# The recurrence's level products, on diagonal blocks of 32 instead of 64

## The reference

```python
def step(S, inp):
    r_t, w_t, k_t, v_t, kk_t, b_t = inp
    sa = jnp.einsum('bhvk,bhk->bhv', S, kk_t)
    S = (S * w_t[:, :, None, :] - sa[..., None] * b_t[:, :, None, :]
         + v_t[..., None] * k_t[:, :, None, :])
    return S, jnp.einsum('bhvk,bhk->bhv', S, r_t)
```

## Time and profile before

| | us |
|---|---|
| median of 3 runs | 3751.14 |
| their range | 3749.05 to 3752.72 |
| the profiled execution's own time | 3751.76 |
| its span, first to last instruction | 3749.9 |
| recurrence, within the span | 821 to 1520 |
| PE busy in the span | 3507.7 |

### The profile page before, as it was taken

The page is one execution under the profiler, slowest core; times in us unless marked ns, Lnnn a source line. Parts: engine busy times, 40 slices in busy tenths (PEclk is TensorE's granted clock), DMA queues, the critical chain, the costliest instruction groups (busy, mean ns, idle before and its releaser), DMA issues.

```text
span 3749.9 us, 63580 instructions
## 1 busy us (share of the span) xinstructions
PE 3507.7 (94%) x28813; PEld 2207.1 (59%) x28813; DVE 1890.8 (50%) x2744; ACT 935.8 (25%) x1858; POOL 49.2 (1%) x114
## 2 busy tenths in 40 slices
PE   7998879989999999799999999998899698999988
PEld 3445655549989898444444444445566345777753
DVE  2038862235555554646555540115999653544524
ACT  3005630125455545220000000100111302233310
POOL 2000000000000000100000000000000000000000
PEclk9999989989999999899999999999999899999999
DMA  6011210000000000222111121113111012010021
GB/s 228 23 42 59 79 68 7 28 6 17 5 18 4 4 4 4 99 84 79 68 62 45 42 92 40 51 56 95 34 34 56 8 66 58 23 34 23 1 84 62
DMA packets 110624, 177.52 MB, mean 47 GB/s; under 512 B 5379, under 2 KB 66562, under 8 KB 109714
## 3 DMA queue, kind: packets, MB, share of 16 engines
q1 hardware_dynamic: 101218, 141.59, 11.2%
q10 hardware_dynamic: 9136, 31.87, 2.4%
HBM read 147.23 MB, written 26.21 MB: 46 GB/s over the span
## 4 chain that ended last, share of the span: by engine, by line
PE 85%; DVE 9%; ACT 3%; DMA 2%; issue 1%; ACTq 0%; SPq 0%; DVEq 0%
PE psum_all L66 84%; ACT sbuf_all L75 3%; DVE sbuf_all L102 3%; DVE sbuf_all L94 3%; DVE sbuf_all L84 2%; PE psum_all L69 1%; ACT L75 1%; DMA sbuf_all<-in_w_mod 1%; DVE sbuf_all L91 0%; DMA sbuf_all<-in_gla_w_out 0%; DVE sbuf_all L108 0%; DVE sbuf_all L90 0%; DMA sbuf_all<-in_w_up 0%; DVE sbuf_all L97 0%; DMA yd_spill<-sbuf_all 0%
## 5 line engine op out<-in xcount | busy, mean ns | idle before, releaser
L66 PE MATMUL psum_all<-sbuf_all 64*64 64x64 f32 (+11 forms) x28042 | 3406.1, 306 | 185.2 <-ACT sbuf_all L75 57.4
L66 PEld LDWEIGHTS psum_all<-sbuf_all 64*64 64x64 f32 (+5 forms) x28042 | 2120.0, 153 | 1449.7 <-issue 1033.3
L75 ACT ACTIVATE sbuf_all<-psum_all 128x512 f32<-128x512 f32 (+5 forms) x925 | 408.2, 461 | 1562.3 <-PE psum_all L66 1435.7
L94 DVE SCALAR_TENSOR_TENSOR sbuf_all<-sbuf_all 128x1040 f32<-128x1040 f32 (+8 forms) x571 | 623.5, 1094 | 25.3 <-PE psum_all L66 4.9
L84 DVE TENSOR_TENSOR sbuf_all<-sbuf_all 128x512 f32<-128x512 f32 (+10 forms) x593 | 470.3, 817 | 167.6 <-ACT sbuf_all L75 123.6
L75 ACT ACTIVATE sbuf_all<-sbuf_all 128x64 f32<-128x64 f32 (+13 forms) x451 | 260.3, 587 | 855.4 <-DVE sbuf_all L78 354.9
L78 DVE COPY sbuf_all<-psum_all 128x256 f32<-128x256 f32 (+5 forms) x137 | 70.9, 526 | 472.1 <-PE psum_all L66 458.5
L75 ACT ACTIVATE sbuf_all<-psum_all,sbuf_all 128x1280 f32<-128x1280 f32 (+5 forms) x212 | 163.8, 781 | 346.4 <-PE psum_all L66 325.6
L84 DVE TENSOR_TENSOR sbuf_all<-sbuf_all,psum_all 128x512 f32<-128x512 f32 (+3 forms) x160 | 102.0, 640 | 273.6 <-PE psum_all L66 272.5
L108 DVE COPY_PREDICATED sbuf_all<-sbuf_all,psum_all 128x256 f32<-128x256 int32 (+2 forms) x296 | 145.5, 493 | 159.1 <-PE psum_all L66 154.5
L90 DVE TENSOR_SCALAR sbuf_all<-sbuf_all 128x256 f32<-128x256 f32 (+11 forms) x150 | 58.0, 425 | 209.1 <-ACT sbuf_all L75 206.3
(11 more groups left out here) (19 smaller groups left out, 140.5 us busy)
## 6 DMA issues: line engine op xcount, KB each, us to landing
sbuf_all<-in_w_mod SPq DMA_DIRECT2D x12, 2048.0 KB, 8.2
sbuf_all<-in_w_up SPq DMA_DIRECT2D x22, 1024.0 KB, 7.6
sbuf_all<-in_w_in SPq DMA_DIRECT2D x6, 2048.0 KB, 8.4
x_spill<-sbuf_all SPq DMA_DIRECT2D x16, 512.0 KB, 2.9
sbuf_all<-in_conv_w_in SPq DMA_DIRECT2D x16, 512.0 KB, 6.3
sbuf_all<-in_gla_w_in SPq DMA_DIRECT2D x8, 1024.0 KB, 5.3
sbuf_all<-in_w_down SPq DMA_DIRECT2D x4, 1792.0 KB, 7.4
hid_spill<-sbuf_all ACTq DMA_DIRECT2D x9, 512.0 KB, 2.6
```

Of the source, the lines that this page charges most:

```text
L66: return self.e.matmul(out, lhsT, rhs, start=start, stop=stop, skip_group_check=True)
L75: return self.e.activation(out, in_, func, bias=bias, scale=scale, **kw)
L94: return self.e.scalar_tensor_tensor(out, a, s, b, op0, op1) if self.e is not None else Unissued()
```

## The change

The first product of levels 1 to 4 is no longer issued as one product of 64 by 64 by 64 for each half of the partitions, but as one of 32 by 32 by 32 for each quarter: the diagonal blocks alone. The rest of the bank is left as it was. Level 5 stays as it is. The planner's time for `level_y` at levels 1 to 4 goes from 500 to 300 ns, which it uses for all three orders.

```diff
+QUARTERS = [(slice(32 * n, 32 * n + 32), 32 * (n % 2)) for n in range(4)]
...
-            step("t", 500, ("level_y", gi, li), ("first_out", gi) if li == 1 else ("de_out", gi, li - 1))
+            step("t", 500 if last else 300, ("level_y", gi, li), ("first_out", gi) if li == 1 else ("de_out", gi, li - 1))
...
             for u in range(4):
-                for rows in HALVES:
-                    done = te.matmul(bank[rows, u * C:(u + 1) * C], g["A"][rows, u, 0:64], g["D"][rows, u, :])
+                if li < SCAN_LEVELS[-1]:
+                    for rows, b in QUARTERS:
+                        done = te.matmul(bank[rows, u * C + b:u * C + b + 32], g["A"][rows, u, b:b + 32], g["D"][rows, u, b:b + 32])
+                else:
+                    for rows in HALVES:
+                        done = te.matmul(bank[rows, u * C:(u + 1) * C], g["A"][rows, u, 0:64], g["D"][rows, u, :])
```

## The result

The kernel with the change takes 3780.19 us (median of 4 runs, 3776.66 to 3788.96) against 3750.33 us (4 runs): a ratio of 1.0079, with a 95% interval of 1.0065 to 1.0093. It is 30 us slower. The forecast was 3755, with a range of 3731 to 3793, and the prediction gave "slower" a chance of 0.45. The time lies in the range, but by luck: what made the kernel slower is a term that the sum does not have, and it was not one of the rivals.

A forecast was written before the change was run, and what follows sets the result against it. The prediction took the PE queue in the recurrence to bound the kernel. Blocks -33.6, shape changes +35.0 and order +1 made +2.4 us on 3751.8, rounded to 3755 us, with a range of 3731 to 3793.

The forecast's parts named there:

- slower: Whole kernel slower by more than the 0.2% (7.5 us) that a measurement tells from no change: chance 0.45.
- Time of a quarter block: Level 1 to 4 blocks on PE: 256 ns instead of 466, saving 33.6 us over 160 blocks.
- The first rival: Four strips don't run side by side: 3788 us at 58 ns per strip (chance 0.17), 3862 taking turns (0.08).
- Round trip between shapes: PE drains and open weight loads around a quarter block: 0.26 us a trip, 144 trips, 35.0 us added after 2.4 off.
- The failed step: PE queue in the recurrence: a nanosecond added or taken goes almost one for one to the end.
- The order: All three queues reordered by the planner's new time: +1 us, ends -24 and +24; more stalls 0.13, fewer 0.11.
- the stall: PE waits 4.2 us for ACT's table loads, then runs at half clock: 8.1 us each, three such stretches.
- Sum: Whole kernel: -33.6 for blocks, +35.0 for shape changes, +1 for order, so +2.4 us on 3751.8 us.
- the wrong mechanism: Four strips on PE not running side by side, for which nearly doubled instructions per time was an argument: chance 0.25.
- other rivals: Slower cases: strips at 58 ns each, 3788 us, chance 0.17; one to three more ACT stalls, 3763 to 3779, 0.13.

The follow-up runs named there:

- half the calls: Quarter products in the old order, but 8 calls to a block, each with a moving operand of two chunks: 3754.76 us, ratio 1.0011 to the kernel before.
- old order: The change's quarter products with the planner's time left at 500, so queues are ordered as in the kernel before: 3788.00 us, ratio 1.0094 to that kernel.
- half the calls issued twice: The kernel of half the calls with each quarter block issued twice, old order: 3799.59 us, ratio 1.0124 to the kernel before.

## Why the prediction was right or wrong

- *Time of a quarter block* (32 ns a record and strip, four strips side by side, 256 ns): right. The first rival priced strips that don't run side by side; they do, and 3788 for it would have been near the measured time for the wrong reason.
- *Round trip between shapes* (0.26 us): right, +0.06 us per block net where +0.05 was worked out. That TensorE drains at a change of tiling mode (the Trainium skill, TensorEngine Tiling, Key Properties) holds for 64 by 64 to 32 by 32 too: the 0.15 us ahead of the block. Block and trips together, forecast at -33.6 + 35.0 = +1.4, are the +3.9 us of half the calls.
- *The failed step*: "a nanosecond added to or taken from the PE queue inside the recurrence goes almost one for one to the end". That took the queue as always full. The sum had counted 2560 records and as many weight loads more and given them no price beyond their own time; the price is 37 - 4 = 33 us in the old order, less 24 ns × 160 = 4 us for the longer block, so 29 us. By the traces about 15 us of it (19.3 - 3.9) are stops at the seams of instruction packets, each ended by a packet's landing. The other part is the lower clock, up to 17 us between the two profiled executions, which differ by 39 us where the medians differ by 33. Why the clock is lower is open. In the trace of after five of the eight stretches at half level have no wait of PE in them or in the 5 us ahead of them; the longest in the quarter products' old order, 20.5 us from 1352.9, lies in 33.66 us in which PE is never idle; and half the calls issued twice has 72.4 us at half level with 8 stops. The prediction had the clue, that instructions per time would nearly double, under the wrong mechanism.
- *The order*: costed at +1 with ends of ±24; it is -12.5 us. Mechanism and size of the stall fit (the 4.2 us stops go, the clock rises); which way it would go could not be read from the trace.
- *Sum*: +2.4 forecast. Measured are +3.9 for half the calls, 4 for the longer block, 29 for the additional instructions, 5 more for the quarter products in the new order than in the old (10 blocks share their changes of shape with a neighbour there and not 16, which is 1.6 us, and the seams lose 7 us more by the traces), and -12.5 for the order: the 30. That 3780 lies in the range is luck: the new order took back part of a price that nobody had counted, and the upper end was there for other rivals.

## What to carry to other kernels

An instruction has a price apart from the time it executes: where an engine already goes through its queue about as fast as the queue is filled, more instructions cost time, however well the pieces run in parallel. A change of array shape is a second price, and here it had already taken all that the smaller products save. Look at the trace for stops with nothing to wait for at equal counts of instructions, and divide the instructions of a stretch by its time before adding any. In a stage that one engine bounds, try the order first: numbers in a planner made this kernel 23 us faster, the arithmetic that the change saves did not.

## What the runs showed of the hardware

PE's instructions arrive in packets of 256 (16.4 KB), each of which took 0.9 to 1.5 us in the stage of after. Where PE stood waiting at the seam, it went on 1.25 to 1.58 us after the landing, and in the rows shown 128 matmul records and 128 weight loads took 3.73 to 4.01 us, 14.6 to 15.7 ns an instruction; over all neighbouring stops in that trace it is 3.47 to 4.03 us.

Four strips of 32 by 32 each take a record every 32 ns or so, and the four start 7 ns apart. A change of array shape costs 0.10 us into the new shape and 0.09 back, for each pair of shapes looked at (64 by 64 with the gate products, the key-spread products and 32 by 32), plus a weight load in the open of 0.8 ns a column.
